# A new hand-written order for the eight heads of a differential-attention stage

## What is computed

```
h = _rms(x, mix_norm)
rq, rk, rv, rg, dq, dk, dv, mq, gates = split(h @ w_in)
dq = rope_partial(_rms(dq.reshape(B, S, 8, 2, 64), diff_q_norm))      # dk likewise
for i in range(4):                       # 128 queries at a time, keys up to the block's end
    s = einsum(q[q0:q1], k[:q1]) / 8     # for both pairs r = 0, 1
    p = softmax(where(mask, s, -inf))
    a = p[:, :, 0] - lam * p[:, :, 1]
    out_i = a @ v[:q1]
do = _rms(do, diff_subln) * (1 - lam_init); diff_out = do @ diff_w_o
g = sigmoid(gates + b_gate)
merged = g[0] * ret_out + g[1] * diff_out + g[2] * mem_out
```

## Time and profile before

| | |
|---|---|
| median of 3 runs | 3380.01 us (3375.14 to 3380.74) |
| the profiled execution | 3380.74 us |
| its span | 3378.9 us |
| TensorE busy | 3229.7 us, 96% |
| VectorE busy | 1212.8 us, 36% |
| ScalarE busy | 1231.6 us, 36% |
| GpSimd busy | 1740.8 us, 52% |
| mean granted clock of TensorE | 0.976 of 2.4 GHz |
| the chain that ended last | 86% TensorE, 8% VectorE |

### The profile page before, as it was taken

One profiled execution on the slowest core, in us unless ns is written; L12 is line 12 of the kernel. 1 busy time (PEld: TensorE's weight loads), 2 busy tenths in 40 slices (PEclk: granted clock), 3 DMA queues, 4 the chain that ended last, 5 costly groups with the idle time before them and its releaser, 6 DMA issues.

```text
span 3378.9 us, 40102 instructions
## 1 busy us (share of the span) xinstructions
PE 3229.7 (96%) x15078; PEld 2631.2 (78%) x15078; DVE 1212.8 (36%) x2152; ACT 1231.6 (36%) x2217; POOL 1740.8 (52%) x1347
## 2 busy tenths in 40 slices
PE   8999999999999999999999898999999887899998
PEld 7888788877777787888887787877888665778886
DVE  3322322214555433232214755524112555231124
ACT  4333333333444435332234323244333344443333
POOL 6555655456454464565555223156556441475563
PEclk9999999999999999999999899999999998999999
DMA  4333322222222232333333112022333220223332
GB/s 157 100 97 94 91 78 81 76 85 77 60 63 63 78 108 83 93 95 103 97 97 84 38 41 60 26 76 87 94 100 100 65 67 26 66 87 97 97 103 72
DMA packets 149839, 275.58 MB, mean 82 GB/s; under 512 B 16528, under 2 KB 17808, under 8 KB 149520
## 3 DMA queue, kind: packets, MB, share of 16 engines
q1 hardware_dynamic: 149648, 273.02, 27.4%
HBM read 270.86 MB, written 2.10 MB: 81 GB/s over the span
## 4 chain that ended last, share of the span: by engine, by line
PE 86%; DVE 8%; POOL 2%; ACT 2%; issue 2%; DMA 0%; SPq 0%; DVEq 0%; ACTq 0%; POOLq 0%
PE PS L477 84%; PE PS L544 2%; DVE AR L1079 1%; POOL SM L2188 1%; DVE TMP L1079 1%; POOL WL L2188 1%; DVE AL L1079 1%; DVE HL L1085 1%; DVE TMP L1085 1%; DVE AR L1085 1%; DVE ACC L1085 1%; DVE SM L1079 1%; POOL TMP L2188 1%; DVE X L1079 0%; DVE SM L1764 0%
## 5 line engine op out<-in xcount | busy, mean ns | idle before, releaser
L2188 POOL TENSOR_TENSOR WL<-RAW,WH 128x512 fp32r<-128x512 f32 x1002 | 1302.0, 1310 | 1042.7 <-ACT WH L1804 1042.1
L1804 ACT ACTIVATE WH<-RAW 128x512 fp32r<-128x512 f32 x1002 | 619.5, 627 | 1088.1 <-PE PS L477 1036.3
L477 PE MATMUL PS<-HH,WH 128*128 128x512 f32 x2296 | 915.2, 399 | 11.0 <-ACT WH L1804 7.7
L477 PE MATMUL PS<-HL,WH 128*128 128x512 f32 x2296 | 903.3, 393 | 7.9 <-DVE HL L1085 6.4
L477 PE MATMUL PS<-HH,WL 128*128 128x512 f32 x2296 | 902.6, 393 | 2.2 <-POOL WL L2188 2.2
L477 PE MATMUL PS<-AH,WH 128*128 128x512 f32 (+1 forms) x1504 | 588.3, 391 | 8.3 <-ACT AH L1804 7.5
L477 PE MATMUL PS<-AL,WH 128*128 128x512 f32 (+1 forms) x1504 | 585.3, 389 | 10.0 <-DVE AL L1079 10.0
L477 PE MATMUL PS<-AH,WL 128*128 128x512 f32 (+1 forms) x1504 | 583.7, 388 | 0.7 <-POOL WL L2188 0.7
L477 PEld LDWEIGHTS PS<-HH,WH 128*128 128x128 f32 x2296 | 436.0, 190 | 104.7 <-ACT WH L1804 8.2
L477 PEld LDWEIGHTS PS<-HL,WH 128*128 128x128 f32 x2296 | 436.2, 190 | 104.3 <-DVE HL L1085 12.0
L477 PEld LDWEIGHTS PS<-HH,WL 128*128 128x128 f32 x2296 | 435.5, 190 | 96.2 <-POOL WL L2188 4.2
(11 more groups left out here) (208 smaller groups left out, 2588.2 us busy)
## 6 DMA issues: line engine op xcount, KB each, us to landing
RAW<-in_wst SPq DMA_DIRECT2D x1002, 256.0 KB, 2.6
X<-in_x SPq DMA_DIRECT2D x8, 256.0 KB, 5.4
TMP<-in_p SPq DMA_DIRECT2D x8, 256.0 KB, 3.1
out<-X SPq DMA_DIRECT2D x8, 256.0 KB, 2.0
AR<-in_dm SPq DMA_DIRECT2D x1, 1024.0 KB, 6.9
AR<-in_mem SPq DMA_DIRECT2D x1, 1024.0 KB, 5.9
CST<-in_cst SPq DMA_DIRECT2D x1, 964.0 KB, 7.8
AR<-in_pos SPq DMA_DIRECT2D x2, 256.0 KB, 2.9
```

What stands on the lines that cost most here:

```text
L477: return e.matmul(o, l, r, start=a, stop=z, skip_group_check=True)
L1804: return e.activation(o, a, f, **kw)
L2188: return e.tensor_tensor(o, a, b, op)
```

## The change

Only the list of steps changes, and the waits that go with it. The scores no longer come in pairs: each `d_sc h q` is followed by a step that prepares the next head (`d_q n 0` behind score 0, `d_q n 1` behind score 1, `d_v n` behind turn 0, `d_vt n` behind score 2, `d_n n` ahead of score 3, `d_rope n 0` ahead of softmax 3, `d_rope n 1` behind turn 2). The next head is then ready before turn 3 and `d_pv`. The fillers are dealt out anew: 1 in head 0 (the first of its four stand ahead of the head), 4 in heads 1 to 3, 2 in heads 4 and 5, 1 in head 6, 3 gates and 3 `mq` in head 7. The whole list of a head such as head 4 is now

```
--- before.py
+++ after.py
@@ -206,30 +206,33 @@
 
 
 def plan_diff():
-
-
-    wide = [x for m in range(8) for x in (("g", 0, m), ("r_out", 3, m))] + [("g", 1, m) for m in range(8)] + [("mq", m) for m in range(3)]
-    p = [("d_q", 0, 0), ("d_q", 0, 1), ("d_v", 0), ("d_vt", 0), wide.pop(0), ("d_n", 0), wide.pop(0), ("d_rope", 0, 0), ("d_rope", 0, 1),
-         wide.pop(0)]
+    gated = [x for m in range(8) for x in (("g", 0, m), ("r_out", 3, m))]
+    g1 = [("g", 1, m) for m in range(8)]
+    mq = [("mq", m) for m in range(8)]
+    fills = [gated[4 * h:4 * h + 4] for h in range(4)] + [g1[0:2], g1[2:4], g1[4:5], g1[5:8] + mq[0:3]]
+    p = [("d_q", 0, 0), ("d_q", 0, 1), ("d_v", 0), ("d_vt", 0), fills[0].pop(0), ("d_n", 0), fills[0].pop(0), ("d_rope", 0, 0),
+         ("d_rope", 0, 1), fills[0].pop(0)]
     for h in range(8):
-        n, nxt, f = h + 1, h < 7, wide[3 * h:3 * h + 3]
-        before = f[:2] if f[0][0] == "r_out" else f[:1]
-        between, behind = f[len(before):2], f[2:]
-        p += [("d_sc", h, 0)] + ([("d_t1", h - 1)] if h else []) + [("d_sc", h, 1)]
-        p += ([("d_q", n, 0)] if nxt else before) + [("d_sm", h, 0)] + ([("d_t2", h - 1)] if h else [])
-        p += [("d_sc", h, 2), ("d_turn", h, 0), ("d_sm", h, 1)]
-        p += ([("d_q", n, 1)] if nxt else between) + [("d_sc", h, 3), ("d_turn", h, 1), ("d_sm", h, 2)]
-        p += ([("d_v", n), ("d_vt", n)] if nxt else behind) + [("d_turn", h, 2), ("d_sm", h, 3)]
-        if nxt:
-            p += before + [("d_turn", h, 3), ("d_n", n)] + between + [("d_pv", h), ("d_rope", n, 0), ("d_rope", n, 1)] + behind
-        else:
-            p += [("mq", 3), ("d_turn", h, 3), ("d_pv", h)]
-    return p + [("mq", 4), ("d_t1", 7), ("mq", 5), ("d_t2", 7)]
+        n, f = h + 1, fills[h]
+        prep = [("d_q", n, 0), ("d_q", n, 1), ("d_v", n), ("d_vt", n), ("d_n", n), ("d_rope", n, 0), ("d_rope", n, 1)] if n < 8 else []
+
+        def some(src):
+            return [src.pop(0)] if src else []
+
+        p += [("d_sc", h, 0)] + some(prep) + ([("d_t1", h - 1)] if h else []) + ([] if prep else some(f)) + [("d_sm", h, 0)]
+        p += [("d_sc", h, 1)] + some(prep) + ([] if prep else some(f)) + ([("d_t2", h - 1)] if h else []) + [("d_sm", h, 1), ("d_turn", h, 0)]
+        p += some(prep) + ([] if prep else some(f))
+        p += [("d_sc", h, 2)] + some(prep) + [("d_sm", h, 2), ("d_turn", h, 1)] + some(f)
+        p += some(prep) + [("d_sc", h, 3)] + some(f)
+        p += some(prep) + [("d_sm", h, 3), ("d_turn", h, 2)] + some(prep) + some(f)
+        p += [("d_turn", h, 3)] + some(f) + [("d_pv", h)] + f
+    return p + [("mq", 3), ("d_t1", 7), ("mq", 4), ("d_t2", 7)]
 
 
 def plan_mem():
     p = [("mload",)] + [("mg", 1, m) for m in range(8)]
-    p += [("mp", m) for m in range(5)] + [("mq", 6)] + [("mp", m) for m in (5, 6, 7)] + [("mq", 7)]
+    p += [("mp", m) for m in range(3)] + [("mq", 5)] + [("mp", m) for m in range(3, 6)] + [("mq", 6)]
+    p += [("mp", m) for m in (6, 7)] + [("mq", 7)]
     p += [("mkl", 0), ("nqm",), ("fac", "nmem"), ("mkl", 1), ("bc", "nmem"), ("mk", 0), ("mk", 1), ("mqn", 0)]
     for m in range(2, 8):
         p += [("mkl", m), ("mk", m)] + ([("mqn", m // 2)] if m % 2 else [])
@@ -1373,9 +1376,7 @@
                 elif kind == "mq":
                     m = i[0]
                     e.wait_ge(*at("mm", "mq", m))
-                    if m == 3:
-                        e.wait_ge(*at("mm", "d_sc", 7, 3, 1))
-                    elif m in (0, 5):
+                    if m in (0, 3):
                         e.wait_ge(*at("mm", "d_pv", 6 if m == 0 else 7))
                     tt(ar(MQS[m]), psum("mq", m), RB, MUL).then_inc(*up("mq", m))
                 elif kind == "mg":
```

## The result

The changed kernel takes 3415.76 us (median of 4 runs, 3411.19 to 3417.19), the kernel before in the same comparison 3380.38 us. The ratio is 1.0105, with a 95% interval of 1.0088 to 1.0122: 35 us slower. The forecast was 3430, slower, in a range from 3388 to 3450. The profiled execution has a span of 3412.8 us against 3378.9, 33.9 more.

What follows compares the result with a forecast made beforehand. TensorE, in order, was taken as the bound. Idle 55.8 less 23.0 winnable gave +32.8 us, the clock 17.6: 50.4 on the profiled 3380.7, 3431.1, median 0.7 lower: 3430, range 3388 to 3450.

Steps and rivals of the forecast that it cites:

- Removed waits: Before turn 0 in each of eight heads: TensorE's waits of about 0.9 us for the probability tile go.
- Query 5: Memory branch's query 5, moved behind the merges: its 5.44 us are the same work, no gain, no loss.
- The chain to softmax 3: VectorE, ScalarE and GpSimd queues after the wide copies: turn 3 may start 11.9 to 18.9 us after W.
- the rival that GpSimd doesn't block: Late filler's panels split earlier, cosine 0 ready, turn 3 at W + 12.2 in heads 1 to 6: +10, 3390 us; chance 0.13.
- The waits before turn 3: TensorE waits for a probability tile: one of 4 to 8 us in each of heads 0 to 6, longest in 4 and 5.
- W: End of the two wide copies in each head: F + 5.8 us, bounds 5.8 and 6.9.
- The path through the heads: Score 0 to the value product's end: 41.6 us in head 0, 51.4 in 1 to 3, 49.6 in 4 and 5, 43.4 in 6.
- The clock: Behind the idle stretch before turn 3 in heads 0 to 6, TensorE at half clock: 17.6 us, bounds nothing and 20.
- The rival of a full clock throughout: The clock never falls, only the idle time counts: +32.8 us, 3413; chance 0.13.
- The idle time: TensorE idle in the stage of the eight heads: from 21.3 us to 55.8.
- The rest: Everything outside the stage of the eight heads: as before.
- Dearer tables: Rival: the table switch before score 3's exponential costs 1.28 us more in heads 1 to 6, 7.7 in all: 3438; chance 0.05.

Runs made afterwards that it cites:

- the experiment with softmax 0: Kernel before the change, with softmax 0 one step earlier, ahead of the next head's query projection: 3370.23 us, ratio 0.9973 of before.
- The experiment on GpSimd's order: Changed kernel, with GpSimd's two cosine products of the next head issued at score 3, ahead of the late filler's panels: 3385.93 us, 1.0023 of the kernel before.
- that on softmax 3: Changed kernel, with softmax 3 one step earlier in the list, ahead of rope 0, in every head: 3393.95 us, 1.0051 of the kernel before.
- the experiment that keeps TensorE at work: Changed kernel, with 2 to 5 products that nothing reads before turn 3 in heads 0 to 6: 3400.62 us, 1.0071 of the kernel before.
- three such moves: Kernel before, with softmax 0 ahead of the query projection, softmax 3 ahead of the value projection, turn 3 directly behind turn 2: 3352.7 us, ratio 0.9917.

## Why the prediction was right, and where it was off

The direction, the place and the mechanism were right. The size was too large: 50.4 us were forecast for the profiled execution and 33.9 measured. Both terms of the sum, the idle time and the clock, were too large.

*Removed waits.* Right: no wait before turn 0, worth 7.3 us by the experiment with softmax 0. Query 5: nothing, as said.

*The chain to softmax 3.* Right item for item: two table loads more in six of the heads (28 where 16 were), the exponentials of score 3 behind one, ScalarE's rounding behind them, GpSimd's split behind that, the cosine product behind the split, VectorE's addition drawn out beside the second cosine product. The experiment on GpSimd's order shows that link as a cause (30 us come back), and that on softmax 3 the link on VectorE; the rival that GpSimd doesn't block is out. What the table loads and exponentials by themselves cost no run separates; they set the wait in head 6. From the end of the wide copies to turn 3 it was 1099.50 - 1081.73 = 17.8 us in head 5, where 18.4 was forecast. The waits before turn 3 were shorter than the 4 to 8 us named: 2.1 in head 0, 4.4 in heads 1 to 3, 5.6 in heads 4 and 5, 3.9 in head 6.

*Where the first size was off: W.* W is the end of the two wide copies, F the end of the value projection, and the prediction put W at F + 5.8, with 5.8 as the lower bound. In head 5 it was 1077.05 to 1081.73, 4.7. Both of its bounds come from heads in which a GpSimd split stood beside the factor. This is VectorE's multiply of 128x16 in head 0 of the kernel before, and GpSimd's power with the split behind it:

```profile
833.89 1.26 DVE L1079 TENSOR_TENSOR SM<-SM 128x16 f32<-128x16 f32 x1 [3.01 <-POOL SM L2188]
```

```profile
830.96 2.89 POOL L2188 TENSOR_TENSOR SM<-SM,VC 128x16 f32<-128x16 f32 x1 [1.25 <-DVE SM L1082]
833.82 1.30 POOL L2188 TENSOR_TENSOR WL<-RAW,WH 128x512 fp32r<-128x512 f32 x1
```

The multiply took 1.26 us there and 0.17 in head 5 after (1080.34). The prediction had said that no split stands in this place in the new order, and yet kept a duration that contained the wait for one: 1.1 us too much in each of seven heads.

*The path through the heads.* The time from a head's score 0 to the next one's goes through three parts: to W, from W to turn 3, and from turn 3 on. In us, forecast (without any fall of the clock) and found, read in each head as in head 5, where the three parts end at 1081.73, 1099.50 and 1105.28 and the head starts at 1055.00:

| head | to W | W to turn 3 | behind turn 3 |
|---|---|---|---|
| 0 | 25.4, 24.4 | 11.9, 11.4 | 4.3, 5.5 |
| 1 | 26.9, 25.6 | 18.9, 19.3 | 5.6, 8.3 |
| 2 | 26.9, 25.6 | 18.9, 19.3 | 5.6, 7.1 |
| 3 | 26.9, 25.6 | 18.9, 19.3 | 5.6, 7.0 |
| 4 | 26.9, 25.6 | 18.4, 17.8 | 4.3, 5.7 |
| 5 | 26.9, 26.7 | 18.4, 17.8 | 4.3, 5.8 |
| 6 | 26.9, 25.6 | 12.2, 11.8 | 4.3, 6.4 |
| sum | 186.8, 179.0 | 117.6, 116.7 | 34.0, 45.7 |

The first column is 7.8 us shorter than forecast: 9.0 less the 1.2 by which the slow stretch of head 4 reached into head 5. Of the 9.0, W's 1.1 per head makes 7.7. The second column is right to 1 us in sum.

*The clock.* Forecast were 17.6 us, one slow stretch behind each wait before turn 3. In the slices of 1 us the clock lacks 1.7 us there in heads 0, 2 and 3, 3.4 in heads 1, 5 and 6 and 5.1 in head 4, but in heads 4 to 6 a part of it still lies in the wait. On the path the slow stretches cost 11.7 in the third column and that 1.2, so 12.9; the experiment that keeps TensorE at work gives 15 for the whole stage. So this term was some 3 to 5 us too large. The rival of a full clock throughout (3413) lay nearer to the measured time than the forecast, but its mechanism is refuted: the clock did fall in every head from 0 to 6. That its number is so near is luck, as it has W too late by 7.7 us and no price for the clock. The number alone would have taught the wrong thing.

*The idle time.* It was forecast to rise from 21.3 to 55.8 us and rose to 39.8, so it looks 16 us short. Not all of that is time won. At half clock TensorE is also busy for longer where it would otherwise have waited: in head 0 most of rope 0 and rope 1 ran at half clock just ahead of the wait of 2.1 us. The heads 0 to 6 took 341.4 us in all, against 338.4 forecast without any fall of the clock.

*The rest.* 3 us less outside the stage, as much as the clock lacked less there in this execution (70.5 us instead of 73.8); that this is more than chance isn't shown.

*Dearer tables.* The exponential of score 3 started 1.30 us after its table load did (1089.04 to 1090.34), so the load's own time is all that it cost here too. Nor is there a pause ahead of a load: the next one started at 1092.84, when the rounding before it had ended at 1092.82, and the sigmoid behind it at 1094.14. The rule of the Trainium skill, "ScalarE: Activation LUTs", What ACT_TABLE_LOAD costs, of some 2.66 us with a drain, isn't seen in this place.

## What to carry to other kernels

Where all engines walk through one list of steps, moving a step moves it in every queue: look for the item that the bound engine waits for, and then for everything that stands ahead of it on each engine, also what has no dependence on it (here weight panels that are due at a filler's place in the list and that only later steps read). Before reordering a whole stage, write down its few waits and move for each the one item that is late: three such moves gave 27 us where the new list lost 35. A wait of TensorE can cost more than its length, for its clock may fall behind it: in the changed kernel it was down behind each of the waits of 3.9 to 5.6 us, while behind those of about 2 it fell in some places and executions only.

## What the runs showed of the hardware

VectorE's small multiply of 128x16 took 0.17 us with GpSimd idle and 1.26 when a GpSimd split had started just before it. An addition of two 128x512 tiles took 1.73 us when GpSimd's cosine product had started before it. Started just ahead of a GpSimd split it took 0.69, and the split 1.75 instead of 1.3: in these rows the one that came second paid. Behind the idle stretches of 3.9 to 5.6 us of TensorE before turn 3 the granted clock was half each time, and its mean over heads 0 to 6 was 0.91 to 0.97. After waits of 1.7 to 2.7 us it fell in some places and not in others. 27 products which nothing reads, put into the waits before turn 3, made the kernel 15 us faster.
